# Recurrent heads with tokens on partitions: values with a ones column as moving operand, norm along rows, gates' chain moved into the attention

## What is computed

```python
def mlstm_chunkwise(q, k, v, i_pre, f_pre):      # cut; per head, chunks of 64 tokens
    b = jnp.cumsum(jax.nn.log_sigmoid(f_pre)..., axis=-1)
    Dlog = jnp.where(lower, b[..., :, None] - b[..., None, :] + i_pre[..., None, :], -jnp.inf)
    m_t = jnp.maximum(m_inter, jnp.max(Dlog, axis=-1))
    S = jnp.einsum('bhntd,bhnsd->bhnts', q, k) * jnp.exp(Dlog - m_t[..., None])
    num = jnp.einsum('bhnts,bhnse->bhnte', S, v) + ...      # what earlier chunks carry
    den = jnp.sum(S, axis=-1) + ...
    h = num / jnp.maximum(jnp.abs(den), jnp.exp(-m_t))[..., None]

def hybrid_mixer(h, w_in, b_in, conv_w, conv_b, rpb, ml_norm_w, w_out):     # cut
    qk = jax.nn.silu(centred_short_conv(jnp.concatenate([ml_q, ml_k], axis=-1), conv_w, conv_b))
    ...
    hm = (h_fwd + h_bwd).transpose(0, 2, 1, 3) * jax.nn.sigmoid(ml_o)...
    mu = jnp.mean(hm, axis=-1, keepdims=True)
    var = jnp.mean(jnp.square(hm - mu), axis=-1, keepdims=True)
    hm = ((hm - mu) * lax.rsqrt(var + EPS)).reshape(B, T, ML_W) * ml_norm_w
    ml_out = hm * jax.nn.silu(ml_z)
    return jnp.concatenate([na_out, ml_out], axis=-1) @ w_out
```

## Time and profile before

| what | us |
|---|---|
| median of 3 runs | 1230.73 (1229.04 to 1234.65) |
| the profiled execution, its own time | 1231.37 |
| its span | 1229.3 |
| of it: attention C ends at | 975.6 |
| scores of heads 0, 1, 2, 3 start at | 1031.4, 1064.7, 1099.8, 1139.4 |
| output projections end at | 1206.4 |

### The profile page before, as it was taken

One profiled execution on the slowest core, in us unless ns is written; L12 is line 12 of the kernel. 1 busy time (PEld: TensorE's weight loads), 2 busy tenths in 40 slices (PEclk: granted clock), 3 DMA queues, 4 the chain that ended last, 5 costly groups with the idle time before them and its releaser, 6 DMA issues.

```text
span 1229.3 us, 19724 instructions
## 1 busy us (share of the span) xinstructions
PE 1141.2 (93%) x7368; PEld 914.6 (74%) x7368; DVE 811.1 (66%) x1579; ACT 648.5 (53%) x1316; POOL 351.3 (29%) x194
## 2 busy tenths in 40 slices
PE   4899999999998899999999999999899978999886
PEld 0588778787885788877778787988777766777565
DVE  6365766667668336455777786468677584897865
ACT  4614555555556337535776677465666444454523
POOL 1532111111111326563000013055322036342731
PEclk9899999999999999999999999999999999999899
DMA  9631434323103111232212210432123015215102
GB/s 355 249 140 44 173 107 167 112 95 111 37 10 139 55 49 52 86 120 54 61 29 84 78 44 2 156 87 63 36 90 125 19 33 173 44 60 155 52 1 69
DMA packets 35146, 111.17 MB, mean 90 GB/s; under 512 B 4500, under 2 KB 7060, under 8 KB 34668
## 3 DMA queue, kind: packets, MB, share of 16 engines
q1 hardware_dynamic: 35052, 109.92, 27.2%
...
## 4 chain that ended last, share of the span: by engine, by line
PE 65%; DVE 20%; ACT 6%; issue 4%; DMA 3%; POOL 1%; SPq 0%; DVEq 0%; POOLq 0%; ACTq 0%
PE PS L642 27%; PE PS L625 13%; PE PS L758 7%; PE PS L746 6%; PE PS L992 3%; DMA AF<-wstream 2%; DVE AF L2241 2%; DVE AD L2180 2%; PE PS L677 2%; PE PS L935 2%; PE PS L841 1%; PE PS L658 1%; PE PS L978 1%; ACT AF L1203 1%; DVE AF L1852 1%
## 5 line engine op out<-in xcount | busy, mean ns | idle before, releaser
L642 PE MATMUL PS<-AR 128*128 128x512 f32 (+1 forms) x2304 | 480.7, 366 | 15.1 <-POOL AR L2317 5.9
L642 PEld LDWEIGHTS PS<-AR 128*128 128x128 f32 x2304 | 387.4, 192 | 88.0 <-issue 21.5
L2317 POOL TENSOR_TENSOR AR<-AF,AR 128x1024 fp32r<-128x1024 f32 x99 | 242.1, 2452 | 683.7 <-ACT AR L1080 683.7
L625 PE MATMUL PS<-AR 128*128 128x256 f32 (+4 forms) x1284 | 247.1, 329 | 15.8 <-POOL AR L2404 5.5
L625 PEld LDWEIGHTS PS<-AR 128*128 128x128 f32 (+1 forms) x1284 | 182.0, 192 | 53.5 <-issue 22.2
L1212 ACT ACTIVATE AF<-PS 128x512 f32<-128x512 f32 (+3 forms) x192 | 124.5, 649 | 115.4 <-PE PS L746 111.5
L1203 ACT ACTIVATE AF<-PS,AF 128x512 f32<-128x512 f32 (+3 forms) x192 | 140.8, 734 | 21.5 <-DVE AF L2159 12.3
L746 PE MATMUL PS<-AF 128*128 128x128 f32 x864 | 128.1, 276 | 8.5 <-DVE AF L1852 4.9
L746 PEld LDWEIGHTS PS<-AF 128*128 128x128 f32 x864 | 100.2, 141 | 33.6 <-issue 15.2
L758 PE MATMUL PS<-AF 128*64 128x128 f32 x1728 | 116.0, 279 | 2.6 <-DVE AF L1859 2.6
L1873 DVE CUSTOM_DVE_ANT_0 PS<-PS,AF 128x512 f32<-128x512 f32 (+2 forms) x96 | 68.4, 714 | 73.6 <-PE PS L625 72.5
(11 more groups left out here) (194 smaller groups left out, 1241.8 us busy)
## 6 DMA issues: line engine op xcount, KB each, us to landing
...
```

The costliest lines, as they stand in the source:

```text
L625: mm = pe.matmul(out, stationary, moving, start=i == 0, stop=i == len(products) - 1)
L642: mm = pe.matmul(out[:, 0:t1 - t0], a, b, start=k == 0 and i == 0, stop=k == nk - 1 and i == 2)
L2317: pool.tensor_tensor(w[:, 1, :], raw(c), w[:, 0, :].bitcast(F32), ALU.subtract).then_inc(lo_done, 1)
```

## The change

- `weigh_head` has the operands the other way round. The weighted scores of a key tile and one token tile (128 by 128) are stationary, and the moving operand is the values with a column of ones behind each head's 128 (MV, 129 wide). Numerator and denominator come out together, tokens on partitions, two token tiles in a bank: ten matmuls a way (only the tiles of the triangle). The scores are kept as a packed triangle (`scored`).
- `divide` works on denominators of 128 by 4, and exp(-m) is now a column for each token tile (EMCOL): the gates' rows GX are transposed next to GI (16 small transposes instead of 8), and ACT takes exp of 128 by 32. The rows that go through DRAM are the negated maxima alone, 512 KB a head.
- The output gate is computed by token for all heads at once (`values_by_token(..., what="o")`, 96 matmuls after D.gcol) instead of four projections in the heads; ACT's tanh for it comes before the first head.
- The norm runs along the row: `centre` sums with a TENSOR_REDUCE, ACT squares four tiles of 128 by 128 with an accumulated sum each, root and Newton step are 128 by 4. The matmuls with `ones` go. `turn_head` transposes the normed head back (four transposes), and `turned_head` on DVE multiplies with the weight and gate z out of PSUM. On ACT, squares and root of head h-1 now stand ahead of `decay(h, 1)`.
- The gates' chain moves into attention C: D.gate is a filler of pair 1's empty step 3, D.q0 and D.k0 are the last pair's. ACT takes softplus in step 5 (`log_gates`), DVE does its pieces in steps 3, 7, 11 and 12 (`gates`). The rows' round trip through DRAM stands ahead of chunk D.o1.

```diff
 def fillers_c(p, step):
     if p == N_NA:
-        return ["D.gate.x", "D.q0.x"][step:step + 1]
-    return [f"C.q{p}.x", f"C.k{p}.x", f"C.z{p}.x"][step:step + 1]
+        return ["D.q0.x", "D.k0.x"][step:step + 1]
+    return [f"C.q{p}.x", f"C.k{p}.x", f"C.z{p}.x", *(["D.gate.x"] if p == 1 else [])][step:step + 1]
...
             values_by_token("D", range(QT), range(4))
-            project("D.k0.x", "D.k0", HC, 0, S)
             out = acc_open("D.gcol")
             pe.wait_ge(gates_max, 1)
...
+            values_by_token("D", range(QT), range(4), what="o")
...
                 for i, j in enumerate(key_tiles(way)):
                     pe.wait_ge(pm_ready, 8 * h + 4 * way + i + 1)
                     t0, t1 = reach(way, j)
-                    for name, acc, stationary in zip(names, outs, (MV[:, j, h * P:h * P + P], ones)):
-                        mm = pe.matmul(acc[:, t0:t1], stationary, PM[:, way, j, t0:t1], start=i == 0,
-                                       stop=i == QT - 1, skip_group_check=True)
+                    for t in range(t0 // P, t1 // P):
+                        at = (P + 1) * (t % 2)
+                        mm = pe.matmul(outs[t // 2][:, at:at + P + 1], scored(way, j)[:, t * P - t0:t * P + P - t0],
+                                       MV[:, j, h, :], start=i == 0 and t % 2 == 0, stop=j == t, skip_group_check=True)
...
+            def turn_head(h):
+                out = acc_open(f"D.turn{h}")
+                pe.wait_ge(dn_ready, h + 1)
+                for t in range(QT):
+                    mm = pe.transpose(out[:, t * P:t * P + P], DV[:, t * P:t * P + P], ident)
...
             for h in range(N_ML):
-                project(f"D.o{h}.x", f"D.o{h}", HC, 0, S)
                 project(f"D.z{h}.x", f"D.z{h}", HC, 0, S)
...
-                if h >= 1:
-                    head_matmul(f"D.mu{h - 1}", hm_ready, h, HM)
                 weigh_head(h, 0)
...
                 if not last:
                     project(f"D.k{h + 1}.x", f"D.k{h + 1}", HC, 0, S)
-                    weigh_head(h, 1)
+                    if h >= 1:
+                        turn_head(h - 1)
+                weigh_head(h, 1)
+            turn_head(N_ML - 2)
             output(0, 0, KD - 2)
             output(1, 0, KD - 2)
-            head_matmul(f"D.mu{N_ML - 1}", hm_ready, N_ML, HM)
             output(2, 0, KD - 2)
-            head_matmul(f"D.var{N_ML - 1}", sqd_ready, N_ML, SQD)
+            turn_head(N_ML - 1)
...
+                if m - B_END == 5:
+                    log_gates()
...
                 act.wait_ge(dv_ready, h + 1)
-                act.activation(SQD, DV, ACT.Square).then_inc(sqd_ready, 1)
+                for t in range(QT):
+                    ins = act.activation(SQD[:, t * P:t * P + P], DV[:, t * P:t * P + P], ACT.Square,
+                                         accum_out=HEAD_SQ[:, t:t + 1])
...
             for h in range(N_ML - 1):
                 output_gates(h)
-                decay(h, 1)
                 if h >= 1:
                     centred_squares(h - 1)
+                    head_root(h - 1)
+                decay(h, 1)
...
+                elif i == 7:
+                    dve.wait_ge(gates_log, 1)
+                    step(dve.scalar_tensor_tensor(GL[0:4], GF[0:4], 0.0, GL[0:4], ALU.min, ALU.subtract))
+                    for way in range(2):
+                        step(dve.tensor_tensor_scan(along(GX, way), one, along(GL, way), 0.0, ALU.mult, ALU.add))
...
-                step(dve.scalar_tensor_tensor(T1, acc, -1.0, RB[:, h % 2, 1, way], ALU.mult, ALU.max))
-                read(dve.tensor_tensor(T1, acc, T1, ALU.max), den)
-                step(dve.reciprocal(T1, T1))
-                read(dve.tensor_tensor(T2 if way else HM, wait_acc(num), T1, ALU.mult), num)
+                step(dve.scalar_tensor_tensor(d, den, -1.0, floor, ALU.mult, ALU.max))
+                step(dve.tensor_tensor(d, den, d, ALU.max))
+                step(dve.reciprocal(DENOM, DENOM))
+                ins = dve.tensor_tensor(by_token(T2 if way else HM), acc[:, :, :, 0:P], each_token(DENOM), ALU.mult)
...
+                step(dve.tensor_reduce(HEAD_SUM, HM.rearrange("p (t n) -> p t n", n=P), AX, ALU.add))
...
-                if name == "D.q1":
-                    sp.wait_ge(rows_ready, 1)
-                    sp.dma_start(rows_dram.rearrange("a d h t -> h a d t"), ROWS[0:4]).then_inc(rows_stored, 16)
+                if name == "D.o1":
+                    sp.wait_ge(gates_max, 1)
+                    sp.dma_start(rows_dram[1].rearrange("d h t -> h d t"), GF[0:4]).then_inc(rows_stored, 16)
                     sp.wait_ge(rows_stored, 16)
```

305 lines of the change are left out of this document (177 added, 128 removed).

## The result

The changed kernel takes **1220.1 us** (median of 5 runs, 1215.7 to 1220.8) where the kernel before takes 1230.6 (5 runs on the same chip): a ratio of 0.9905, with a 95% interval from 0.988 to 0.993. (The ratio is estimated from all runs; the two medians alone give 0.991.) The forecast was 1194 with a range of 1183 to 1209. The direction was right, but only 10.5 of the 36 us came. The profiled execution took 1220.81 us, its span 1219.0.

What follows compares the result with a forecast made beforehand. PE and DVE were both taken as near the bound. Attention +5.6, stage to the first scores -2.7, heads' loops -26.0 and last stage -13.2 sum to -36.3 us, giving 1194 us, range 1183 to 1209.

Steps and rivals of the forecast that it cites:

- What bounds the kernel: Before the change, PE (busy 93% of the span) and DVE are both near the bound, so a change must shorten both.
- The work removed: In the heads' loop: DVE loses 6.4 us of reciprocals, gains 0.7 of row sum; PE's work falls from 35 to 24.9.
- A way of `weigh_head`: One weighing of a head on PE: ten matmuls of 129 columns take 2.4 us instead of 4.32, upper bound 3.8.
- The rival on loads: Weight loads not hidden behind streaming make a weighing way 3.8 us; the kernel takes 1200 us; chance 0.09.
- The heads' loops: From one head's scores to the next's: 25, 28.5 and 28.5 us, 82 instead of 108.0, so -26.0.
- The last stage: Last scores to the outputs' end: outputs begin at 13.2 us, stage 53.8 instead of 67.0, so -13.2.
- The attention: Attention C, to 975.6: D.k0 as added PE filler costs +5.6 us, the gates' chain on DVE nothing.
- I take 0 with this cover: In the attention, PE's fillers of 5.6 us hide DVE's gates' pieces; without this cover the whole 12.4 us is paid.
- POOL costs 10 to 30 us of the gain: In the heads, POOL's splits hold up DVE's operations with two operands in SBUF; 10 to 30 us lost; chance 0.05.
- The gates' rival: In the attention, step 7's 5.7 us on DVE delay the next maxima: +7 us, 1201 us; chance 0.14.
- PE as the bound: In the heads' loop PE's 24.9 us sets the pace: 82 becomes 75, the time 1185 us; chance 0.12.
- Signs: Wrong if: weighing record above 0.15 us, PE waiting around fillers or for D.o1, small DVE operations above 0.3, taps above 1.3.

Runs made afterwards that it cites:

- run with narrow lows: Changed kernel with POOL writing the low parts of later weight chunks and the outputs' right-hand sides in 16 columns only, just to measure: 1197.9 us.
- best version: Changed kernel with POOL's list in the heads and the last stage reordered and the gates' step 7 piece cut in three, nothing left out: 1197.7 us.
- the two runs: Changed kernel with the gates' step 7 piece spread over steps 6, 9, 10 (1219.0 us), or over 9, 10, 11 with the rest behind the attention (1219.6 us).

## Why the prediction was wrong

**What bounds the kernel: half right.** It said that PE and DVE are both near the bound and that the chain DVE, ACT, POOL is next. It was next at once: PE is busy for 26 of 33 us in a loop, and 17 us of added matmuls cost nothing.

**The work removed: right.** The reciprocal takes 0.18 us (0.16 forecast), the row sum 0.69, PE's busy time in a loop 23.8 to 26.6 (24.4 and 24.9 forecast, the rest at half clock). DVE waits 1.90 us for ACT in front of the second weighing, where 3 was counted, and the two old waits of the norm went.

**A way of `weigh_head`: right.** Forecast 2.4, bounds 2.2 and 3.8. It takes 2.15 from start to start, 0.1075 us a record:

```profile
1111.38 2.39 PE L992 MATMUL PS<-AF 128*128 128x129 f32 x20
1113.53 5.72 PE L659 MATMUL PS<-AR 128*128 128x512 f32 x24
```

The rival on loads (3.8 a way) falls. The Trainium skill's figure for a load of 128 columns (page TensorE: Matmul & The Clock Gate, section LDWEIGHTS), 107 ns, gives an estimate of 2.1 us for 20 loads, and the trace agrees; but the columns' own 2.2 fits as well, so no run here shows which of the two sets the pace.

**The heads' loops, the step that failed (12.6 of the 26 us).** The sentence was "and the convolutions as they are in the mean (0.945 a tap)". The mean of the old heads mixed taps of 0.78 with blocked ones, and the step assumed that the same share would be hit. Measured over heads 1 and 2:

```profile
L2242 DVE SCALAR_TENSOR_TENSOR AD<-AD,AF 128x512 f32<-128x512 f32 x16 | 19.9, 1246 | 0.8 <-DVE AF L2317 0.3
```

1.246 a tap, eight taps a head: 2.4 us more than counted, and 1.9 on `centre`, that the sum had at its bare 0.69. Together 4.3 a head, against a loop that came out 4.3 longer than the 28.5 forecast. That these agree to the tenth is luck, for three smaller terms lie beside them: the Newton operation at 2.31 (1.1 a head in the mean) was not counted, ACT's wait was counted 1.1 too high, and the old loops, from which the sum started, held 0.9 a head of the same blocking in an operation that the prediction never looked at, the sum of both ways at 1.6 instead of 0.69:

```profile
L2244 DVE TENSOR_TENSOR AF<-AF 128x512 f32<-128x512 f32 x2 | 3.2, 1599 | 0.1
```

In the run with narrow lows the taps are at 0.87 in the mean. With that, ACT's wait at 1.9 and the old blocking out, the forecast's sum would be 28.5 - 0.6 - 1.1 - 0.9 = 25.9, and the run has 26.7 and 27.1. So the rest of the sum held to about 1 us a head, which stays unplaced. In the first loop the same kind of loss, 3.7 (28.9 against 25.2), was not counted at all.

**The last stage (8.5).** The outputs were to begin at 13.2 and began at 20.1. Of the 6.9 the Newton step is the largest part, 4.0: its four operations were counted at 0.16 and took 1.1 to 1.2, because ACT's six copies let loose POOL's six lows at that very moment. `centre(2)`, done at 4.8 instead of 3.5, and `finish`'s last operation, 1.72 instead of 0.69, are the next. The best version, with the lows put elsewhere, begins at 13.7. In the outputs themselves PE lost some 1.5 at half clock (14.02 for 54 matmuls that take 12.52 in the best version) and 1.9 in front of head 3's turn, where 1 was allowed for; the first two operations of that Newton step took 2.28 and 1.20 beside POOL's chunks.

**The attention (6.6).** "I take 0 with this cover" failed. 1.0 us of the 12.2 lies ahead of it (the values' stage began at 819.7 instead of 818.7), which is no effect of the edit: in the other runs, the same up to there, it began between 817.2 and 820.0. PE's wait for pair 2's gate rose from 0.8 to 3.5, and all of these 2.6 is the gates' piece of step 7, as the timelines of the two runs show: it took 3.7 us, less than the 5.7 counted, but it pushes the mask of pair 3, and with it that gate, back. What faced PE's filler was not this piece alone but the piece with the mask, 3.7 + 3.9 us. The matmuls behind the wait went at half pace. At the end of the attention POOL's splits of D.v chunks came in for the first time:

```profile
981.96 2.60 DVE L1888 TENSOR_SCALAR AF<-AF 128x512 f32<-128x512 f32 x1
```

```profile
981.92 2.35 POOL L2392 TENSOR_TENSOR AR<-AF,AR 128x1024 fp32r<-128x1024 f32 x1 [0.94 <-ACT AR L1097]
```

The normalising takes 0.49 without POOL beside it; this one took 2.60 and the one before it, beside the split at 978.61, 1.63, and PE waited 1.2 and 1.0 for them. The prediction counted PE's added filler there, and not these splits. That the two waits go with the splits was not tried. 1.0, 2.6 and 2.3 leave 0.7 of the 6.6, about the size of the matmuls at half pace.

**The rivals and the chances.** The case that came true was on the list: "POOL costs 10 to 30 us of the gain", with 0.05. Its mechanism, its operations and even its price for one encounter (2.0 for a split on four taps) stood in the text. What was missing was the count. The text named 12 to 14 us of POOL's work in a head and left 0.05 for the case that 3 to 10 us of it meet an operation that it can block. On a chain that had just been cut from 35 to 28 us, with the blockable operations nearly all still in it, that was the likely case. The gates' rival was right in kind and less than half in size (2.6 us of wait and some of the 0.7, where it had 7). PE as the bound fell. The direction is no proof of the mechanism: the work removed was worth 24.8 us where POOL is out of the way, and POOL's work took 14 of them back.

**Signs.** One sign of being wrong on the list came true: small DVE operations above 0.3 us (2.31 in a head, 1.1 to 2.3 in the last stage). Another, taps above 1.3 in the mean, did not, since they came out at 1.25, with the forecast already lost: it was set too high, since 0.3 more a tap is 2.4 us a head. PE's waits around the fillers were for the gate of a pair and not for the maxima.
